# Forgetting attention in a hybrid encoder step: scores of two heads on the two halves of the array rows, transposed, in rounded passes

## The chip, the cores and the metric

The kernel runs on one core of a Trainium2 chip. The metric is the device time of one execution in microseconds (us). The engines are named as in the profile: PE (matrix multiply), PEld (its weight loads), DVE (vector), ACT (activations), POOL, and SP, whose queue issues most transfers.

## The reference

One inference step of a one-layer encoder over 1024 prompt frames and 64 sample frames (width 1024). An RMS norm and one input projection feed two attention groups; their outputs are normalised, projected, added to the input, and followed by a mixture of experts (32 experts, top 2 of one group of 8). All of it is float32. The change touches the first group, forgetting attention with 8 heads of dimension 64:

```python
c_k = jnp.cumsum(logf, axis=1).transpose(0, 2, 1)
sc = (jnp.einsum('bqhd,bkhd->bhqk', qi, k) * SCALE + ci[..., None] - c_k[:, :, None, :])
sc = jnp.where(kpos[None, :] <= qpos[:, None], sc, -jnp.inf)
pr = jax.nn.softmax(sc, axis=-1)
o = jnp.einsum('bhqk,bkhd->bqhd', pr, v)
```

The sample's 64 frames see 256 cached frames and themselves, with the same formula. The outputs of the kernel include the projected K and V.

## The kernel before, in words

Frames are laid out in tiles of 128 partitions: eight prompt tiles (0 to 7), the sample tile (8, half filled), and two tiles of cached keys (9, 10). The kernel has stages that follow one another on PE: input projection in nine column groups of 256 (L1435, three float32r products of high and low parts), forgetting attention (L1484 to L1581), window attention (from L1587), output projection, router, experts.

Forgetting attention loops over pairs of heads (`pe.Fori`, L1570), within a pair over 18 steps, each one query tile of one head. The keys of a head are staged: POOL copies q and k of one head into `qst` and `kst` (L504 to L509), with a 65th column that holds 1/SCALE for q and minus the cumulative log-forget for k, so that the product contains the key's bias. PE transposes them (L1511; the first head L1484), ACT copies the q tiles out of PSUM (L691) and DVE the k tiles (L1039).

A step has six parts. PE multiplies q by all keys up to the diagonal in full float32 (`fqk`, L1530) and adds the causal mask with a bf16 product (L1533); each step alternates between two PSUM couples of banks. DVE takes the negated row maximum (L1047). ACT computes the exponential into `prob` and the row sum (L714). PE transposes each 128x128 block of probabilities (`ftrans`, L1546), DVE copies the first four blocks (L1052) and ACT the others (L724) into `probT`. PE multiplies them by V into one sum over the keys (`fpv`, L1566). DVE scales by the reciprocal of the row sum (L1056, L1059).

Each engine has a queue of its own, in a written order, and waits on semaphores. PE's order within step k is: scores of step k+1, a staging group of the next head, transposes of step k, values of step k-1. The scores of a query tile with n key blocks need 2n instructions' worth of columns, since a float32 product is two instructions.

On SP's queue: cached keys and values arrive once the eighth column group is done (L352 to L355), K and V go out after the projection (L362 to L376), and `w_out` is loaded (L381) when all values have been multiplied and the outputs have left.

Of the kernel before, what the change touches and what calls it, by code (L numbers as in the profile page):

```python
# [6 lines left out]
F32 = mybir.dt.float32  # L7
# [18 lines left out]
SWA = NH * DH + 2 * 2 * DH  # L26
PROJ = QKV + NH + SWA
# [15 lines left out]
def build(nc, t):  # L43

    ctx = ExitStack()
    with ctx:
# [37 lines left out]
        kT = [cut(big, free0 + u * NK * P, NK * P) for u in range(2)]  # L84
        qT = [cut(big, free0 + 2 * NK * P + u * NT * P, NT * P) for u in range(2)]
        at = free0 + 2 * NK * P + 2 * NT * P
        prob = [cut(big, at + u * SEQ, SEQ) for u in range(2)]
        probT = [cut(big, at + (2 + u) * SEQ, SEQ) for u in range(2)]
# [49 lines left out]
        for name in ("e", "s", "r", "a", "hid", "hidT"):  # L138
# [19 lines left out]
        fox_t = fox[:, 0:NT * QKV].rearrange("p (t n) -> p t n", t=NT)  # L158
# [21 lines left out]
        wg_hi = [rounded("wg_hi0", fox_at, NT * QKV, C, WG), rounded("wg_hi1", work_at, 2 * D, C, WG)]  # L180
# [5 lines left out]
        ck = cut(work, at, 2, (NH + 1) * DH)  # L186
        at += 2 * (NH + 1) * DH
        cv = cut(work, at, 2, NH * DH)
        at += 2 * NH * DH
        kst = cut(work, at, NK, DH + 1)  # L190
        at += NK * (DH + 1)
        qst = cut(work, at, NT, DH + 1)
        at += NT * (DH + 1)
        skv = cut(work, at, 2 * 2 * DH)
        at += 2 * 2 * DH
        assert at <= 4 * D
        sqst = cut(work, at, NT, P)
        at += NT * P
        assert at <= 6 * D
        at = NT * QKV + C * WG  # L200
        lz = cut(fox, at, 3 * NT * NH)
        at += 3 * NT * NH
        lsum = cut(fox, at, NK * NH)
        lsum_t = cut(fox, at, NK, NH)
        assert at + NK * NH <= NT * QKV + WSLOT
# [29 lines left out]
        negc = sb("negc", [P, NK * (NH + 1)])  # L235
# [19 lines left out]
            pad_set aug_set kv_staged st_T st_copied_s st_copied_v qk_done nmax_done exp_done pT_a pT_b cp_a cp_b pv_done o_done recip  # L255
# [4 lines left out]
            v_idx v_g v_w v_gT v_gTc v_gu v_e v_s v_hid v_hT v_hTc v_dn v_y v_out experts_done  # L260
# [19 lines left out]
        def wg_dest(g, i):  # L280

            to, c0 = (fox_t, g * WG) if g < FOX_G else (swa_t, (g - FOX_G) * WG)
            return to[:, i, c0:c0 + WG]
# [9 lines left out]
        nblk = [i + 1 for i in range(NP_T)] + [1 + PAST // P]  # L293
        TWO = [i for i in range(NT) if nblk[i] > 4]

        SG = [("q", 0, 4), ("q", 4, 8), ("q", 8, 9), ("k", 0, 4), ("k", 4, 8), ("k", 8, 11)]
        SG_AT = {2: 0, 3: 1, 4: 2, 5: 3, 6: 4, 7: 5}
# [4 lines left out]

        def keytile(i, b):

            return b if i < SAMPLE else [NT, NT + 1, SAMPLE][b]
# [8 lines left out]
        def _(sp):  # L314
# [37 lines left out]
            sp.dma_start(ck[:, :, 0:NH * DH], t["cache_fox_k"].rearrange("l b (t p) h d -> p (l b t) (h d)", p=P)).then_inc(s["cache_in"], 16)  # L352
            sp.dma_start(cv[:, :, :], t["cache_fox_v"].rearrange("l b (t p) h d -> p (l b t) (h d)", p=P)).then_inc(s["cache_in"], 16)
# [6 lines left out]
            for n, name in ((1, "fox_k"), (2, "fox_v")):  # L360
                cols = slice(n * 512, (n + 1) * 512)
                sp.dma_start(t[name + "_prompt"].rearrange("l b (t p) h d -> p (l b t) (h d)", p=P),  # L362
                             fox_t[:, 0:NP_T, cols]).then_inc(s["kv_out"], 16)
                sp.dma_start(t[name + "_sample"].rearrange("l b s h d -> (l b s) (h d)"),
                             fox_t[0:DEC, SAMPLE, cols]).then_inc(s["kv_out"], 16)
# [1526 lines left out]
```

## Time and profile before

| | us |
|---|---|
| median of 3 runs | 1003.92 (1002.94 to 1005.01) |
| the profiled execution's own time | 1010.65 |
| its span in the profile | 1008.8 |
| PE busy / DVE / ACT / POOL in the span | 890.9 / 480.2 / 320.5 / 104.8 |
| forgetting attention, 264 to 472 us | 208 |

The span is the time between the first and the last instruction of the profiled execution. Busy times count overlapping matmuls once. The granted clock is the share of full speed (2.4 GHz) that PE was given; in any moment it is either 1.2 or 2.4 GHz, and a stretch shows the mean.

### The profile page before, as it was taken

How to read it: one execution, taken by the hardware profiler on the slowest of the kernel's cores; microseconds unless marked ns; L12 is line 12 of the kernel's file. 1: busy time of each engine (PE TensorE's matmuls, PEld its weight loads, DVE VectorE, ACT ScalarE, POOL GpSimd, SP SyncE). 2: the span in 40 equal slices, each digit the busy share in tenths (PEclk: the TensorE clock that was granted, in tenths of full speed). 3: DMA queues.
4: the chain of work that ended last, by engine and by line, in shares of the span. 5: the costliest groups of instructions: out<-in, count | busy, mean ns of one | idle time of the engine just before them, and what ended most of it. 6: DMA issues, size and time to landing. Idle time of an engine off the chain costs nothing.

```text
span 1008.8 us, 16897 instructions
## 1 busy us (share of the span) xinstructions
PE 890.9 (88%) x5891; PEld 777.5 (77%) x5891; DVE 480.2 (48%) x1058; ACT 320.5 (32%) x800; POOL 104.8 (10%) x188
## 2 busy tenths in 40 slices
PE   4999999999999999997999989999649999999700
PEld 4999999999787878786989878888537777777400
DVE  4631111111465656666676743342354555544366
ACT  5621111110333443442555733332202222222222
POOL 0000000000000000010000000000132443333200
PEclk9999999999999999999998989999659999999955
DMA  9301111111500000002100042211668999982195
GB/s 260 128 2 42 42 42 42 42 42 48 205 4 1 0 0 0 0 0 90 78 1 0 0 168 84 84 62 73 236 240 309 356 333 323 336 318 101 54 372 179
DMA packets 50699, 118.45 MB, mean 117 GB/s; under 512 B 12960, under 2 KB 22944, under 8 KB 50656
## 3 DMA queue, kind: packets, MB, share of 16 engines
q1 hardware_dynamic: 41440, 100.03, 27.8%
q0 software_dynamic: 9216, 17.85, 5.1%
q8 instruction: 27, 0.44, 0.2%
q14 instruction: 16, 0.13, 0.0%
HBM read 102.93 MB, written 30.64 MB: 132 GB/s over the span
## 4 chain that ended last, share of the span: by engine, by line
PE 83%; DVE 8%; DMA 4%; ACT 2%; issue 2%; SPq 0%; DVEq 0%; POOLq 0%; ACTq 0%; POOL 0%
PE ps L1435 32%; PE ps L1765 11%; PE ps L1530 7%; PE ps L1566 7%; PE ps L1771 6%; PE ps L1546 3%; PE ps L1758 3%; PE ps L1617 3%; PE ps L1650 2%; PE ps L1511 2%; PE ps L1708 2%; DMA out_y_prompt<-big 1%; PE ps L1679 1%; PE ps L1634 1%; DVE big L1403 1%
## 5 line engine op out<-in xcount | busy, mean ns | idle before, releaser
L1435 PE MATMUL ps<-wg_hi,xl 128*128 128x256 f32 x576 | 163.3, 284 | 0.2 <-DVE wg_lo L948 0.2
L1435 PE MATMUL ps<-wg_lo,xh 128*128 128x256 f32 x576 | 163.0, 283 | 0.0
L1435 PE MATMUL ps<-wg_hi,xh 128*128 128x256 f32 x576 | 163.0, 283 | 0.0
L1435 PEld LDWEIGHTS ps<-wg_hi,xl 128*128 128x128 f32 x576 | 110.6, 192 | 0.4 <-issue 0.4
L1435 PEld LDWEIGHTS ps<-wg_lo,xh 128*128 128x128 f32 x576 | 110.6, 192 | 0.0
L1435 PEld LDWEIGHTS ps<-wg_hi,xh 128*128 128x128 f32 x576 | 110.6, 192 | 0.0
L714 ACT ACTIVATE big<-ps,nm 128x384 f32<-128x384 f32 (+7 forms) x72 | 52.1, 723 | 124.5 <-DVE nm L1047 122.9
L1530 PE MATMUL ps<-big 128*128 128x512 f32 (+3 forms) x224 | 85.0, 493 | 1.2 <-DVE big L1039 0.8
L1566 PE MATMUL ps<-fox,big 128*128 x592 | 75.4, 271 | 1.2 <-DVE big L1059 1.2
L1566 PEld LDWEIGHTS ps<-fox,big 128*128 128x128 f32 x592 | 72.0, 192 | 2.9 <-issue 2.8
L1765 PEld LDWEIGHTS ps<-fox,work 128*128 128x128 f32 x320 | 60.8, 190 | 16.8 <-issue 9.6
L1765 PE MATMUL ps<-fox,work 128*128 128x256 f32 x320 | 72.3, 379 | 0.0
L1047 DVE TENSOR_REDUCE nm<-ps 128x1 f32<-128x384 f32 (+7 forms) x72 | 52.9, 735 | 40.1 <-PE ps L1533 39.8
L1298 DVE COPY work<-ps 128x512 f32<-128x512 f32 x32 | 22.1, 691 | 96.7 <-PE ps L1758 96.7
L952 DVE COPY fox<-ps 128x256 f32 (+1 forms) x27 | 11.4, 422 | 101.8 <-PE ps L1435 101.8
L1435 PE MATMUL ps<-w_out_h,oTl 128*128 128x512 f32 x144 | 57.7, 401 | 1.5 <-DVE oTl L1176 1.5
L1435 PE MATMUL ps<-w_out_h,oTh 128*128 128x512 f32 x144 | 56.7, 394 | 0.0
L1435 PE MATMUL ps<-w_out_l,oTh 128*128 128x512 f32 x144 | 56.6, 393 | 0.0
L1530 PEld LDWEIGHTS ps<-big 128*128 128x128 f32 x224 | 38.4, 198 | 17.6 <-issue 17.1
L1546 PE MATMUL ps<-cf,big 128*128 128x128 f32 x312 | 46.8, 276 | 1.1 <-ACT big L714 1.1
L1617 PE MATMUL ps<-big 128*128 128x128 f32 x272 | 42.0, 301 | 4.8 <-DVE big L1086 4.5
L754 ACT ACTIVATE big<-ps,nm 128x256 f32<-128x256 f32 (+1 forms) x72 | 32.7, 460 | 42.5 <-DVE big L1121 25.6
(236 smaller groups left out, 1650.5 us busy)
## 6 DMA issues: line engine op xcount, KB each, us to landing
fox<-in_w_gate SPq DMA_DIRECT2D x20, 512.0 KB, 4.6
fox<-in_w_up SPq DMA_DIRECT2D x20, 512.0 KB, 7.2
fox<-in_w_down SPq DMA_DIRECT2D x20, 512.0 KB, 6.7
work<-in_w_in SPq DMA_DIRECT2D x8, 1024.0 KB, 5.4
fox<-y_rows SPq DMA_DIRECT2D x16, 512.0 KB, 7.0
h_rows<-big SPq DMA_DIRECT2D x9, 512.0 KB, 2.6
work<-in_x_prompt SPq DMA_DIRECT2D x8, 512.0 KB, 7.0
fox<-in_w_out SPq DMA_DIRECT2D x1, 4096.0 KB, 12.8
```

The source lines that it names most:

```text
L714: act.activation(prob[k % 2][:, 0:n], ps[k % 2][:, 0:n], ACT.Exp, bias=nm[:, k % 2:k % 2 + 1], accum_out=rs[:, k % 4:k % 4 + 1]).then_inc( ...
L754: act.activation(sprob[k % 2][:, v, lo:2 * P], bank[k % 3][:, v * 256 + lo:v * 256 + 256], ACT.Exp, bias=nm[:, 2 * (k % 3) + v:1 + 2 * (k ...
L1047: dve.tensor_reduce(nm[:, k % 2:k % 2 + 1], ps[k % 2][:, 0:n], AX.X, ALU.max, negate=True).then_inc(s["nmax_done"], 1)
L1298: dve.tensor_copy(hgT[u][:, 4:8, :], bank[1].rearrange("p (c k) -> p c k", c=4)).then_inc(s["gT_cv"], 1)
L1435: mm = pe.matmul(out, xs[a](c), ws[b](c), start=(c + k == 0), stop=(c == C - 1 and k == 2))
L1530: pe.matmul(ps[k % 2][:, at_:at_ + w], q, kT[u][:, k0:k0 + w], start=(at_ % 512 == 0), stop=False, skip_group_check=True)
L1546: mm = pe.transpose(bank[4 + b // 4][:, (b % 4) * P:(b % 4) * P + P], prob[k % 2][:, b * P:(b + 1) * P], ident)
L1566: mm = pe.matmul(bank[6][:, (k % 2) * DH:(k % 2) * DH + DH], probT[k % 2][:, b * P:(b + 1) * P], v, start=(b == 0), stop=(b == nb - 1))
L1617: pe.matmul(bank[k % 3][:, v * 256 + b * P:v * 256 + (b + 1) * P], sqT[u][:, i * P:(i + 1) * P], skT[v][:, m * P:(m + 1) * P], start=(v == ...
L1758: mm = pe.transpose(bank[c // 4][:, (c % 4) * P:(c % 4) * P + P], src[:, c, :], ident)
L1765: mm = pe.matmul(bank[2 + u][:, 0:2 * FE].rearrange("p (m f) -> p m f", m=2), hgT[u][:, c, :], wv[:, c, :, :], start=(c == 0), stop=(c == ...
L1771: mm = pe.matmul(bank[4 + n], ex["hidT"][u], w[:, 2 * D + 512 * n:2 * D + 512 * n + 512], start=True, stop=True)
```

## The change

Two heads are now handled together, as a pair. Their q and k, which lie side by side in 128 columns of the projection, are transposed together (20 transposes for a pair), so head 0 of the pair lands on partitions 0 to 63 and head 1 on 64 to 127. ACT copies the PSUM tile to a float32r high part (`high`), DVE subtracts it from the PSUM tile to get the low part (`low`). POOL's staging is gone, and with it the 65th column.

For each pair the scores are computed twice.

The natural pass (`scores`, groups n0 to n12 of the list `NAT`) gives only the row maxima: one float32r product of the high parts for each head on its 64 rows, one product with `sel` and `c_rows` that adds the key's bias, and the mask. It writes to banks 0 and 1, which are its only ones. One DVE reduce takes the maxima of both heads (`fmax`). `make_rows` splits the maxima in high and low parts, PE transposes them (`rows_of_maxima`), and DVE spreads them to rows that a product can add.

The transposed pass (`scores_T`) has keys on partitions and queries along the free axis: per step one key tile against up to four query tiles, low x high, high x low, high x high, then a product of ones with the row of maxima, then the mask. Steps alternate between banks 2, 3 and 4, 5. ACT computes the exponential of it straight into `probT`, with the key's bias as its per-partition bias, so no probability is transposed. V has a 65th column of ones, so that `values` also gives the row sums. Its sums for four query tiles and two heads stay in banks 6 and 7 over one half; a pair has two halves (query tiles 0 to 3 and the sample, then 4 to 7), with 7 and 8 steps.

The list `BESIDE` says what stands on PE between the scores of step j+1 and the values of step j: s0 to s5 are staging groups, n0 to n12 natural groups, r0 and r1 the rows of maxima. In the first half these are of the same pair, in the second half of the next pair.

The biases of the keys reach `c_rows` by 16 small transfers from SBUF to SBUF on SP's queue, one for each head and part. K and V leave by one transfer for each tile, V in pieces of 64 elements. The loops of ACT, DVE and PE in this stage are written out instead of `Fori`, those of ACT and DVE for the projection's column groups too. Four small operations of DVE and five of ACT make constants. In the overflow part of the experts some semaphores are merged; no instruction changes there.

The order and the steps:

```diff
+        NPAIR = NH // 2
+        SG = [("k", 0, 4), ("q", 0, 4), ("k", 8, 11), ("q", 8, 9), ("k", 4, 8), ("q", 4, 8)]
+        NAT = [[(3, 0, 512), (8, 8 * P, 384), (2, 0, 384), (1, 0, 256), (0, 0, 128)],
+               [(7, 0, 512), (7, 512, 512), (6, 0, 512), (6, 512, 384), (5, 0, 512), (5, 512, 256), (4, 0, 512), (4, 512, 128)]]
+        STEP = [[(0, 0, 4), (1, 1, 4), (2, 2, 4), (3, 3, 4), (9, 8, 9), (10, 8, 9), (8, 8, 9)],
+                [(m, max(m, 4), 8) for m in range(8)]]
+        N_SG, N_NAT, N_STEP = len(SG), len(NAT[0]) + len(NAT[1]), len(STEP[0]) + len(STEP[1])
+
+        BESIDE = [[["n5", "n6"], ["n7", "n8"], ["n9", "n10"], ["n11", "n12"], ["r1"], [], []],
+                  [["s0", "s1"], ["s2", "s3"], ["s4", "s5"], ["n0", "n1"], ["n2", "n3", "n4"], ["r0"], [], []]]
```

ACT and DVE:

```diff
+            def fexp(n, hp, half, j, step):
+
+                m, a, b = step
+                act.wait_ge(s["fx_st"], n + 1)
+                if n >= 2:
+                    act.wait_ge(s["fx_pv"], n - 1)
+                for v in range(2):
+                    act.activation(probT[2 * (n % 2) + v][:, 0:(b - a) * P], bank[2 + 2 * (n % 2) + v][:, 0:(b - a) * P], ACT.Exp,
+                                   bias=negc_t[:, m, 2 * hp + v:2 * hp + v + 1], scale=SCALE).then_inc(s["fx_exp"], 1)
+
...
+            def fmax(hp, k):
+
+                half, i, k0, w = nat(k)
+                to = top[0][:, :, slot(0, i)] if half == 0 else top[1][:, k0 // 512, :, slot(1, i)]
+                dve.wait_ge(s["fx_nat"], hp * N_NAT + k + 1)
+                dve.tensor_reduce(to, both[:, :, 0:w], AX.X, ALU.max, negate=True).then_inc(s["fx_max"], 1)
+
+            def make_rows(hp, half):
+
+                g = hp * 2 + half
+                nj = 4 if half else 5
+                dve.wait_ge(s["fx_max"], hp * N_NAT + (N_NAT if half else len(NAT[0])))
+                if half:
+                    small_step(dve.tensor_tensor(top[1][:, 0], top[1][:, 0], top[1][:, 1], ALU.min))
+                val = top[1][:, 0] if half else top[0]
+                small_step(dve.tensor_copy(nm_v[:, :, 0:nj], val))
+                small_step(dve.tensor_tensor(nm_v[:, :, 8:8 + nj], val, nm_v[:, :, 0:nj].bitcast(F32), ALU.subtract))
+                dve.sem_inc(s["fx_rc"], 1)
+                dve.wait_ge(s["fx_nmT"], g + 1)
+                if half == 0:
+                    dve.tensor_scalar(row_s, bank[0][:, 0:P], mask8[:, 4:5], None, ALU.mult)
+                dve.tensor_tensor(rows[half].rearrange("p (j q) -> p j q", q=P), bank[0][:, None, 0:P].to_broadcast([P, 4, P]),
+                                  mask8[:, 0:4, None].to_broadcast([P, 4, P]), ALU.mult).then_inc(s["fx_row"], 1)
```

PE, the new functions and the order:

```diff
+            def scores(hp, k):
+                half, i, k0, w = nat(k)
+                u = hp % 2
+                if k == 0:
+                    pe.wait_ge(s["fx_lo"], (hp + 1) * N_SG)
                 else:
+                    pe.wait_ge(s["fx_max"], hp * N_NAT + k)
+                if k == len(NAT[0]):
+                    pe.wait_ge(s["fx_row"], 2 * hp + 1)
+                half_rows = [slice(64 * v, 64 * v + 64) for v in range(2)]
+                for v, r_ in enumerate(half_rows):
+                    pe.matmul(bank[v][:, 0:w], qh[u][r_, i * P:(i + 1) * P], kh[u][r_, k0:k0 + w], start=True, stop=False,
                               skip_group_check=True)
+                dg = i * P - k0
+                ends = 0 <= dg < w
+                for v, r_ in enumerate(half_rows):
+                    mm = pe.matmul(bank[v][:, 0:w], sel[hp][r_, :], c_rows[r_, k0:k0 + w], start=False, stop=not ends,
+                                   skip_group_check=True)
+                if ends:
+                    for v in range(2):
+                        mm = pe.matmul(bank[v][:, dg:dg + P], identb, causal, start=False, stop=True, skip_group_check=True)
+                mm.then_inc(s["fx_nat"], 1)
+            def rows_of_maxima(hp, half):
+                pe.wait_ge(s["fx_rc"], 2 * hp + half + 1)
+                pe.transpose(bank[0][:, 0:P], nm_st.bitcast(F32), ident).then_inc(s["fx_nmT"], 1)
+            def scores_T(n, hp, half, j, step):
+                m, a, b = step
+                u = hp % 2
+                w = (b - a) * P
+                if n >= 2:
+                    pe.wait_ge(s["fx_exp"], 2 * (n - 1))
+                if j == 0:
+                    pe.wait_ge(s["fx_row"], 2 * hp + half + 1)
+                out = [bank[2 + 2 * (n % 2) + v][:, 0:w] for v in range(2)]
+                half_rows = [slice(64 * v, 64 * v + 64) for v in range(2)]
+                for first, (x_, y_) in enumerate([(kl, qh), (kh, ql), (kh, qh)]):
+                    for v, r_ in enumerate(half_rows):
+                        pe.matmul(out[v], x_[u][r_, m * P:(m + 1) * P], y_[u][r_, a * P:b * P], start=(first == 0), stop=False,
+                                  skip_group_check=True)
+                at_ = (a - 4 * half) * P
+                for v, r_ in enumerate(half_rows):
+                    src = row_s[r_, :] if a == SAMPLE else rows[half][r_, at_:at_ + w]
+                    mm = pe.matmul(out[v], ones_r[r_, :], src, start=False, stop=(a != m), skip_group_check=True)
+                if a == m:
+                    for v in range(2):
+                        mm = pe.matmul(out[v][:, 0:P], causal, identb, start=False, stop=True, skip_group_check=True)
+                mm.then_inc(s["fx_st"], 1)
+            def values(n, hp, half, j, step):
+                m, a, b = step
+                if j == 0:
+                    pe.wait_ge(s["fx_o"], 2 * hp + half)
+                for v in range(2):
+                    pe.wait_ge(s["fx_exp"], 2 * n + 1 + v)
+                    val = fox_v[:, m, 2 * hp + v, :] if m < NT else cv[:, m - NT, 2 * hp + v, :]
+                    for i in range(a, b):
+                        at_ = slot(half, i) * HD
+                        mm = pe.matmul(bank[6 + v][:, at_:at_ + HD], probT[2 * (n % 2) + v][:, (i - a) * P:(i - a + 1) * P], val,
+                                       start=(j == 0 and i == a), stop=(m == i), skip_group_check=True)
+                mm.then_inc(s["fx_pv"], 1)
+            pe.wait_ge(s["pad_set"], 4)
+            pe.wait_ge(s["sel_set"], NPAIR + 1)
+            pe.wait_ge(s["crow_in"], 16 * 2 * NH)
+            for k in range(len(NAT[0])):
+                scores(0, k)
+            rows_of_maxima(0, 0)
+            pe.wait_ge(s["evac_v"], EVAC_V)
+            pe.wait_ge(s["evac_s"], EVAC_S)
+            order = list(steps())
+            scores_T(*order[0])
+            for n, hp, half, j, step in order:
+                if n + 1 < len(order):
+                    scores_T(*order[n + 1])
+                for kind, k, to in beside(hp, half, j):
+                    if kind == "s":
+                        stage(to, k)
+                    elif kind == "n":
+                        scores(to, k)
                     else:
+                        rows_of_maxima(to, k)
+                values(n, hp, half, j, step)
```

SP's queue, the key biases:

```diff
+            sp.wait_ge(s["pad_set"], 2)
+            sp.wait_ge(s["c8_hi"], 1)
+            sp.wait_ge(s["c8_lo"], 1)
+            for h in range(NH):
+                for b, part in enumerate((ch, cl)):
+                    r_ = 64 * (h % 2) + 2 * (h // 2) + b
+                    sp.dma_start(c_rows[r_:r_ + 1, :].bitcast(F32).rearrange("a (t c) -> a t c", c=P),
+                                 part[h * NK:(h + 1) * NK, :].bitcast(F32)).then_inc(s["crow_in"], 16)
```

## Rows read from the trace of the kernel before

**Rows 1.** The page: busy time, share of the span and instructions; and the clock in 40 slices.

```profile
PE 890.9 (88%) x5891; PEld 777.5 (77%) x5891; DVE 480.2 (48%) x1058; ACT 320.5 (32%) x800; POOL 104.8 (10%) x188
...
PEclk9999999999999999999998989999659999999955
```

**Rows 2.** Table of windows: stretch, length, each engine's busy us (instructions), clock, DMA share, GB/s.

```profile
264.00:472.00 208.00, 201.86 (x1392) 162.77 (x1392) 128.59 (x311) 82.31 (x203) 13.82 (x34) 0.98 0.07 24
472.00:583.00 111.00, 98.83 (x771) 92.14 (x771) 82.08 (x256) 63.34 (x227) 5.08 (x8) 0.92 0.11 42
...
735.00:1008.00 273.00, 205.54 (x968) 157.52 (x968) 141.25 (x268) 66.86 (x157) 78.59 (x128) 0.86 0.73 264
```

**Rows 3.** Timeline of PE, 276 to 288 us: start, duration, engine, line, operation, count.

```profile
276.01 1.72 PE L1530 MATMUL ps<-big 128*128 128x512 f32 x4
...
279.79 1.94 PE L1530 MATMUL ps<-big 128*128 128x512 f32 x4
281.56 0.22 PE L1533 MATMUL ps<-cb 128*128 128x128 bf16 x1
281.62 0.60 PE L1511 MATMUL ps<-cf,work 128*65 128x128 f32 x4
...
285.20 1.04 PE L1546 MATMUL ps<-cf,big 128*128 128x128 f32 x8
286.07 1.67 PE L1566 MATMUL ps<-fox,big 128*128 x14
```

**Rows 4.** Chain of waits: start, duration, what, with its count.

```profile
234.16 20.18 PE ps L1435 x168
...
600.91 10.90 PE ps L1435 x48
```

**Rows 5.** Timeline of all engines, two moments; idle time and its releaser in brackets.

```profile
410.00 0.22 PE L1533 MATMUL ps<-cb 128*128 128x128 bf16 x1
...
410.26 1.22 DVE L1047 TENSOR_REDUCE nm<-ps 128x1 f32<-128x1024 f32 x1 [1.20 <-PE ps L1533]
...
467.91 0.28 DVE L1059 TENSOR_SCALAR big<-ps,rc 128x64 f32 x1 [1.21 <-PE ps L1566]
...
468.34 1.97 PE L1566 MATMUL ps<-fox,big 128*128 x16 [0.31 <-DVE big L1059]
```

**Rows 6.** DVE by line and shape, 264 to 472 us: count, busy us, mean ns, idle before.

```profile
L1047 DVE TENSOR_REDUCE nm<-ps 128x1 f32<-128x1024 f32 x8 | 9.8, 1224 | 9.6 <-PE ps L1533 9.6
...
L1047 DVE TENSOR_REDUCE nm<-ps 128x1 f32<-128x768 f32 x8 | 7.7, 958 | 6.6 <-PE ps L1533 6.6
...
L1047 DVE TENSOR_REDUCE nm<-ps 128x1 f32<-128x512 f32 x8 | 5.5, 691 | 1.2 <-PE ps L1533 1.2
...
L1047 DVE TENSOR_REDUCE nm<-ps 128x1 f32<-128x256 f32 x8 | 3.4, 424 | 1.8 <-PE ps L1533 1.4
```

**Rows 7.** ACT by line and shape, 264 to 472 us.

```profile
L714 ACT ACTIVATE big<-ps,nm 128x384 f32<-128x384 f32 x16 | 9.3, 581 | 17.4 <-DVE nm L1047 17.4
...
L714 ACT ACTIVATE big<-ps,nm 128x512 f32<-128x512 f32 x8 | 5.5, 687 | 8.1 <-DVE nm L1047 8.1
L724 ACT ACTIVATE big<-ps 128x512 f32<-128x512 f32 x8 | 4.8, 598 | 0.0
...
L714 ACT ACTIVATE big<-ps,nm 128x256 f32<-128x256 f32 x8 | 3.8, 474 | 12.2 <-DVE nm L1047 10.6 <-PE ps L1546 1.6
...
L714 ACT ACTIVATE big<-ps,nm 128x128 f32<-128x128 f32 x8 | 2.9, 368 | 26.3 <-DVE nm L1047 26.3
```

**Rows 8.** Timeline of SP's queue: transfers that it issues.

```profile
235.23 0.43 SPq L355 DMA_DIRECT2D work<-in_cache_swa_v  x1
262.00 0.33 SPq L359 DMA_DIRECT2D g<-in_g_ffn_norm  x1
...
263.50 1.90 SPq L362 DMA_DIRECT2D out_fox_v_prompt<-fox  x1
```

**Rows 9.** The page's line on DMA packets.

```profile
DMA packets 50699, 118.45 MB, mean 117 GB/s; under 512 B 12960, under 2 KB 22944, under 8 KB 50656
```

More of the change, by code:

```diff
@@ L292, in build, with steps, beside, nat @@
         NS = len(STEPS)
[L293 to L297, printed above, removed]
+        NPAIR = NH // 2
[7 more added lines that the diff above has]
+                  [["s0", "s1"], ["s2", "s3"], ["s4", "s5"], ["n0", "n1"], ["n2", "n3", "n4"], ["r0"], [], []]]
+        def steps():
+            n = 0
+            for hp in range(NPAIR):
+                for half in range(2):
+                    for j, step in enumerate(STEP[half]):
+                        yield n, hp, half, j, step
+                        n += 1
+        def beside(hp, half, j):
+            for what in BESIDE[half][j]:
+                at_ = hp + half
+                if at_ < NPAIR:
+                    yield what[0], int(what[1:]), at_
+        def nat(n):
+            half = 0 if n < len(NAT[0]) else 1
+            return (half,) + NAT[half][n - half * len(NAT[0])]
+        def slot(half, i):
+            return 4 if i == SAMPLE else i - 4 * half
         SSG = [(0, 4), (4, 8), (8, 9)]
@@ L737, in stage_sq @@
+            fexp(*next(steps()))
+            order = list(steps())
+            for n, hp, half, j, step in order:
+                if n + 1 < len(order):
+                    fexp(*order[n + 1])
+                for kind, k, to in beside(hp, half, j):
+                    if kind == "s":
+                        high(to, k)
             def stage_sq(g3, u, gi, bk=7):
@@ new lines, in _ @@
+            for k in range(len(NAT[0])):
+                fmax(0, k)
+            make_rows(0, 0)
+            for n, hp, half, j, step in steps():
+                for kind, k, to in beside(hp, half, j):
+                    if kind == "s":
+                        low(to, k)
+                    elif kind == "n":
+                        fmax(to, k)
+                    else:
+                        make_rows(to, k)
+                if j == len(STEP[half]) - 1:
+                    fnorm(hp, half)
@@ L1490, in _ @@
                 product(k // 2 + 1, k, i).then_inc(s["proj_done"], 1)
+                if i == 3:
+                    pe.wait_ge(s["c_ready"], 1)
+                    pe.transpose(bank[1][0:NH * NK, 0:P], c8[:, :], ident).then_inc(s["c8_T"], 1)
                 if i >= 6:
[L1492 to L1512 removed]
@@ L1570, in _ @@
[L1570 to L1584 removed]
+                    if i == 6:
+                        pe.wait_ge(s["c8_lo"], 1)
+                        pe.wait_ge(s["cache_in"], 16 * 5)
@@ new lines, in _ @@
+            pe.wait_ge(s["pad_set"], 4)
+            pe.wait_ge(s["sel_set"], NPAIR + 1)
+            pe.wait_ge(s["crow_in"], 16 * 2 * NH)
+            for k in range(len(NAT[0])):
+                scores(0, k)
+            rows_of_maxima(0, 0)
+            pe.wait_ge(s["evac_v"], EVAC_V)
+            pe.wait_ge(s["evac_s"], EVAC_S)
+            order = list(steps())
+            scores_T(*order[0])
+            for n, hp, half, j, step in order:
+                if n + 1 < len(order):
+                    scores_T(*order[n + 1])
+                for kind, k, to in beside(hp, half, j):
+                    if kind == "s":
+                        stage(to, k)
+                    elif kind == "n":
+                        scores(to, k)
+                    else:
+                        rows_of_maxima(to, k)
+                values(n, hp, half, j, step)
```

411 lines of the change are left out of this document (159 added, 252 removed).

## The prediction

> **What bounds the kernel now.** The page's busy line and clock line come first: the matmul engine (PE) is busy 88% of the span and no other engine reaches half of it [rows 1]. The table of windows cuts the span into stages: the forgetting attention, which is what changes, lies from 264 to 472 us, and there PE is busy 201.9 of 208 us at a granted clock of 0.98, against DVE 128.6 and ACT 82.3 [rows 2]. So in this stage only two things count: time for which PE is occupied, and time for which it must wait. Everything of ACT, DVE, POOL and the DMA queues counts only through a wait of PE.
>
> A busy figure of PE overlaps itself, since a matmul shows 0.27 us or more while the next one starts much sooner. I therefore price matmuls by their pitch. Eight probability transposes take 1.04 us in all, the first one's 0.27 included, so each further one costs (1.04 - 0.27)/7 = 0.11 us; 14 value matmuls take 1.67 us, also 0.11 each; a full float32 product is two instructions, so a 128-key block of values is 0.22 us; the score line grows from 1.72 to 1.94 us for 128 more keys, 0.22 us a block; the mask matmul lasts 0.22 us but the next one starts 0.06 us after it [rows 3]. The rounded (float32r) products of the projections run at 20.18/168 = 0.120 us for 256 columns, and at 10.92/48 = 0.2275 us for 512 [rows 4]. I take 0.174 us for 384, and for 128 the 0.11 us which every 128-column weight load shows as its floor.
>
> Check on the stage of before: one head has 39 blocks of 128x128 keys by queries, so 39 x 0.22 scores + 9 x 0.06 masks + 39 x 0.11 probability transposes + 20 x 0.11 staging transposes + 39 x 0.223 values = 24.3 us, a pair of heads 48.6; the stage measured 208/4 = 52.0 a pair, 3.4 us of it waits. This is the sum that the new one has to beat.
>
> **The change, for one pair of heads.** Staging: 20 transposes serve both heads, 2.2 us (before: 4.4). The probability transposes (78 x 0.11 = 8.6 us) go, with their copies on DVE and ACT. The values stay: 156 instructions of 0.1115, 17.4 us, only their output is 65 columns for 64. Masks double to 36 at 0.06 = 2.2 us. Two transposes of the maxima are 0.2.
>
> Scores are now computed twice. The natural pass (for the maxima alone) has 13 groups with widths 512 x6, 384 x3, 256 x2, 128 x2: 6 x 0.2275 + 3 x 0.174 + 2 x 0.12 + 2 x 0.11 = 2.35 us for one matmul each, times 2 (scores, then the key bias), times 2 heads = 9.4 us. The transposed pass has 15 steps, 512 x6, 384 x2, 256 x2, 128 x5: 2.50 us, times 4 (three rounded products and the row of maxima), times 2 heads = 20.0 us. Together 29.4 us if each matmul waits its turn. The two heads of a pair, however, lie on array rows 0-63 and 64-127, write to different banks and stand next to each other in the program. No row of this trace has a matmul on half the rows, so the price is bounded: below, both heads in one pitch, 29.4/2 = 14.7 us; above, 29.4. Between them, if the products run side by side but the two weight loads follow one another (2 x 0.11 = 0.22 us a couple): 36 couples at 0.2275 and 50 at 0.22 = 19.2 us. I take 17.0, the middle of 14.7 and 19.2, because disjoint rows leave nothing in the products to share, and only the loads are in doubt. The page TensorEngine Tiling (Array Packing), Key Properties, of the Trainium skill says that tiles on different rows load weights and multiply in parallel; no run here shows it yet, and by it the term would be the 14.7.
>
> Waits inside the pair. The natural pass owns one couple of banks, and PE stands at a natural group until DVE has reduced the previous one. Where two stand in one slot of the written order, nothing covers that. One wait: from the last matmul's issue to the reduce 0.26 us, the reduce itself (now two banks at once, so 2 x 512 = 1024 elements, 1.22 us), and 0.15 us from DVE's end to PE, less the pitch already counted: 1.55 us [rows 5, 6]. By the order this happens before n6, n8, n10, n12 and n1 (1024 elements), n3 (768: 0.96, so 1.29) and n4 (512: 0.69, so 1.02): 5 x 1.55 + 1.29 + 1.02 = 10.1 us. Behind the waiting group on PE stand the values of the current step, so nothing else can run. The one-block steps at the end of the first half add about 0.3: PE has 0.45 + 0.55 us of other work for two exponentials of 0.37 [rows 7] and their hand-overs. 10.4 us.
>
> The other engines stay under PE. ACT: 30 exponentials, 12 x 0.69 + 4 x 0.58 + 4 x 0.47 + 10 x 0.37 = 16.1, and six high parts at 0.6 or less: 19.4 us [rows 7]. DVE: reduces 12.4, low parts about 3.7, norms and rows about 5: 21 us. The wait of staging group 2 for the low part of group 0 comes out covered: about 3.1 us of ACT and DVE against 3.5 us of PE work (transposes 0.9, values 1.8, next scores 0.9). The norm of a half (about 1.4 us) lies under the next scores and two groups.
>
> Pair: 2.2 + 0.2 + 2.2 + 17.4 + 17.0 + 10.4 = 49.4 us; four pairs 197.6.
>
> Beside them. At the start nothing covers the natural groups of pair 0, nor the row chain after them: about 4.6 us more (1.3 for one more bare wait, 2.7 for maxima, transpose and rows, 0.6 for the first exponential). Its staging ends with a copy and then a subtraction where a single copy stood: 1.2 us. At the end the norm has three multiplications of four blocks, 0.8 us. Together 6.6. The 16 small row transfers are issued on SP from about 249 us (their source is ready after five products of 24 x 0.12 us from 234 us on) to 256 us at 0.4 us each, or to 265 us and later where the queue is full and an issue takes 1 to 1.9 us [rows 8]; I cost them at nothing, since the last product runs to 262 us, and at 4 us if the cover fails. The output of V is now 256-byte pieces, over 8,700 where the whole kernel had 12,960 packets under 512 B [rows 9]; only the load of w_out waits for it, 200 us later. POOL's staging goes, which PE did not wait for.
>
> Turning between half-row and full-row products. PE does this about 18 times a pair each way where no wait hides it, 144 in all. The rows show that a matmul's tail past its pitch is 0.22 - 0.06 = 0.16 us [rows 3]; between full-row forms this costs nothing, so the bounds are 0 and 0.16 us, 0 to 23 us in all. I take 0.07, since part of the tail must lie under the next weight load: 10 us. The Trainium skill's page TensorEngine Tiling (Array Packing), Key Properties, also says that a change of tiling mode drains the engine; by it the term would be the 23 us. This is the rule that speaks against the change, and nothing in this trace agrees or disagrees.
>
> Stage: 197.6 + 6.6 + 10 = 214.2 us against 208, so +6.2. The profiled execution of before took 1010.65 us around a span of 1008.8; it would become 1016.9. It lies 6.7 us over the median of the three runs, and I carry the difference over to the median: 1003.9 + 6.2 = 1010 us.
>
> **Rivals.**
> B, faster: loads as well as products of the two heads run side by side, and turning costs nothing. Scores 14.7: stage 4 x 47.1 + 6.6 = 195 us, 13 less than before: 991 us. For it: the two loads touch disjoint rows as the products do, and full-row forms follow each other without a gap in [rows 3]. Against it: every load form here has a floor of 0.11 us, whatever its matmul. It decides for faster as soon as a couple of 128-column products has a pitch near 0.11 us and turning stays under 0.04 us.
> C, no overlap: a half-row matmul costs its full turn. Scores 29.4: 4 x 12.4 = 50 us over the forecast, 1060 us. For it: no row shows an overlap. Against it: separate rows, separate banks, alternating order.
> D, the clock: PE now stands 42 us of the stage in gaps of 1 to 1.6 us. The expert stage, PE 75% busy, has a granted clock of 0.86, the window attention with 89% has 0.92 [rows 2]. At 0.86 the 172 us of PE work in the stage grow by 172 x (0.98/0.86 - 1) = 24 us: 1034 us. Against it: the idle stretches there are longer than any here.
>
> **How the numbers follow.** Forecast 0.45, B 0.28, C 0.17, D 0.10. The forecast's own range takes scores 14.7 to 19.2 and turning 0 to 23 us, without both low ends together: 1000 to 1032. The range takes in B with a few us below it and C's centre: 988 to 1063. This kernel can be told from no change beyond 0.2%, 2 us. Faster: B and 0.06 of the forecast, 0.34; same 0.10; slower 0.56.
>
> **What would show it.** Couples of half-row matmuls that start within some ns of each other confirm the overlap; their pitch at 128 columns (0.11 or 0.22) tells B from the forecast; a step from the first half-row product after values later than 0.11 us shows the turning. PE's waits for the reduce should number 28 with about 40 us in total. The stage should be 214 us long with PE idle some 45 of it. The prediction is wrong if the couples don't overlap (stage over 250), if the waits for the reduce are much shorter than 1.5 us, or if the clock of the stage falls under 0.95.

## The result, and the profile after

The changed kernel takes 1111.0 us (median of 4 runs, 1105.5 to 1114.9) against 1004.5 us of the kernel before (median of 4 runs), a ratio of 1.105 (1.098 to 1.111). The forecast was 1010 us and its range ended at 1063: it was wrong. The profiled execution took 1112.8 us, its span is 1110.9 us.

The page of the changed kernel, to be held against [rows 1]; each digit of the clock line is one slice of 28 us:

```profile
PE 966.6 (87%) x6024; PEld 833.4 (75%) x6024; DVE 428.0 (39%) x880; ACT 306.9 (28%) x744; POOL 91.2 (8%) x154
...
PEclk9999999997575675565558998999985999999965
```

The table of windows for the changed kernel: a stretch of the attention stage at full clock, one at the low clock, two longer ones in which PE never waits, and in the last row the whole stage:

```profile
325.00:328.00 3.00, 3.00 (x27) 2.92 (x28) 1.17 (x2) 2.24 (x4) 0.00 (x0) 1.00 0.03 5
334.00:337.00 3.00, 3.00 (x17) 2.25 (x16) 0.00 (x0) 0.05 (x1) 0.00 (x0) 0.50 0.00 0
343.00:355.00 12.00, 12.00 (x65) 10.46 (x64) 0.98 (x3) 1.47 (x4) 0.00 (x0) 0.50 0.01 1
545.00:578.00 33.00, 33.00 (x158) 28.96 (x158) 0.00 (x0) 7.55 (x14) 0.00 (x0) 0.50 0.00 1
262.00:578.00 316.00, 278.08 (x1522) 219.29 (x1522) 78.15 (x128) 66.78 (x139) 0.00 (x0) 0.58 0.06 17
```

Before, the stage had 208 us at a clock of 0.98 [rows 2]; now it has 316 us at 0.58. The stages behind it last 537 us before and 532 after. So all of the loss is in this stage, and PE runs at 1.2 GHz in most of it; the run with filled waits below shows that nearly all of the loss is this clock. The clock comes back four times, near 318, 356, 390 and 469 us, and after 484 us no more in this stage, though PE is busy without a break in its last 33 us (545 to 578 us, at 0.50). That is why a table of busy time misleads here.

The waits of PE for the reduce in the changed kernel (us in total, times, longest) are 29, the 28 of the forecast and the one more at the start. They sum to 34.9 us where 41.7 were forecast:

```profile
PE ps L1584 <- DVE rs L1093: 21.2, 16, 1.3
PE ps L1584 <- DVE nm L1093: 13.7, 13, 1.3
```

The timeline of PE in the changed kernel shows the same products at both clocks. The two heads' halves are one line, x2:

```profile
325.86 1.90 PE L1635 MATMUL ps<-fox,big 128*128 128x65 f32 x16
327.69 0.50 PE L1614 MATMUL ps<-qh,kl 64*128 64x512 f32 x2
328.03 0.40 PE L1614 MATMUL ps<-ql,kh 64*128 64x512 f32 x2
328.26 0.40 PE L1614 MATMUL ps<-qh,kh 64*128 64x512 f32 x2
...
341.94 3.62 PE L1635 MATMUL ps<-fox,big 128*128 128x65 f32 x16
...
347.05 2.66 PE L1635 MATMUL ps<-fox,big 128*128 128x65 f32 x12
349.64 0.47 PE L1614 MATMUL ps<-qh,kl 64*128 64x128 f32 x2
349.91 0.41 PE L1614 MATMUL ps<-ql,kh 64*128 64x128 f32 x2
350.13 0.41 PE L1614 MATMUL ps<-qh,kh 64*128 64x128 f32 x2
```

At full clock a couple of 512-column halves has a pitch of 0.23 us (328.03 to 328.26), that of one 512-column product [rows 4]: they run side by side. A run of 16 values takes 1.90 us there and 3.62 us at the low clock, a pitch of 0.11 and 0.21 us. Products of 100 columns in place of 65 take nearly the same time in the runs below (16 in 1.98 us at full clock). So the columns do not set this pitch; the load of 128 columns of weights, which is the same for both, is what is left. Such products are called load-bound here, and sparse, because the array has columns to multiply in only a part of each pitch.

### The profile page after: what moved, and what is told of

It is laid out like the page before. It is cut to its first block, busy times and chain, and to the rows that moved or that the text cites. A ratio compares the mean times of both kernels' runs of the same rounds, so it can differ in the third digit from the quotient of the medians.

```text
span 1110.9 us, 15975 instructions
## 1 busy us (share of the span) xinstructions
PE 966.6 (87%) x6024; PEld 833.4 (75%) x6024; DVE 428.0 (39%) x880; ACT 306.9 (28%) x744; POOL 91.2 (8%) x154
## 4 chain that ended last, share of the span: by engine, by line
PE 83%; DVE 9%; DMA 3%; issue 2%; ACT 2%; SPq 1%; DVEq 0%; POOLq 0%; ACTq 0%; POOL 0%
PE ps L1502 29%; PE ps L1635 10%; PE ps L1843 10%; PE ps L1614 6%; PE ps L1849 5%; PE ps L1584 3%; PE ps L1836 3%; PE ps L1695 3%; PE ps L1728 2%; DVE rs L1093 2%; PE ps L1619 2%; PE ps L1786 1%; PE ps L1589 1%; DVE nm L1093 1%; SPq L412 1%
## 5 line engine op out<-in xcount | busy, mean ns | idle before, releaser
L757 ACT ACTIVATE big<-ps,negc 128x512 f32<-128x512 f32 (+3 forms) x120 | 58.1, 535 | 247.7 <-PE ps L1622 169.3
L1635 PE MATMUL ps<-fox,big 128*128 128x65 f32 x592 | 118.2, 375 | 0.0
L1635 PEld LDWEIGHTS ps<-fox,big 128*128 128x128 f32 x592 | 114.0, 291 | 4.6 <-issue 3.9
L1584 PE MATMUL ps<-kh,qh 64*128 64x512 f32 (+3 forms) x104 | 32.5, 622 | 36.9 <-DVE rs L1093 21.2
L1093 DVE TENSOR_REDUCE rs<-ps 128x2 f32<-128x1024 f32 (+3 forms) x32 | 32.8, 1026 | 75.5 <-PE ps L1589 55.1
L1584 PEld LDWEIGHTS ps<-kh,qh 64*128 64x128 f32 x104 | 14.0, 266 | 54.2 <-DVE rs L1093 32.1
L983 DVE COPY fox<-ps 128x256 f32<-128x256 f32 x27 | 11.4, 423 | 100.8 <-PE ps L1502 100.8
L679 ACT ACTIVATE fox<-ps 128x256 f32<-128x256 f32 x27 | 10.4, 386 | 108.2 <-PE ps L1502 108.2
```

What stands on the lines that cost most here:

```text
L757: act.activation(probT[2 * (n % 2) + v][:, 0:(b - a) * P], bank[2 + 2 * (n % 2) + v][:, 0:(b - a) * P], ACT.Exp, bias=negc_t[:, m, 2 * hp ...
L1093: dve.tensor_reduce(to, both[:, :, 0:w], AX.X, ALU.max, negate=True).then_inc(s["fx_max"], 1)
L1584: pe.matmul(bank[v][:, 0:w], qh[u][r_, i * P:(i + 1) * P], kh[u][r_, k0:k0 + w], start=True, stop=False, skip_group_check=True)
L1635: mm = pe.matmul(bank[6 + v][:, at_:at_ + HD], probT[2 * (n % 2) + v][:, (i - a) * P:(i - a + 1) * P], val, start=(j == 0 and i == a), sto ...
```

## The experiments

Theory A: uncovered waits pull the clock down, and the sparse products (values of 65 columns, couples of 128) keep it down. Theory B: products on half the rows, or the mix as such, do it. These kernels answer a question about time; some of them leave out a part of the computation, as said there. In the code, `...` marks lines left out. Each window row shows the stage: length, busy us of PE, PEld, DVE, ACT and POOL, clock, DMA share, GB/s.

**Shorter waits, same products.**

```diff
-                dve.tensor_reduce(to, both[:, :, 0:w], AX.X, ALU.max, negate=True)
+                dve.tensor_reduce(to, both[:, :, 0:32], AX.X, ALU.max, negate=True)
```

> Everything of the changed kernel stays, but DVE reduces only the first 32 columns of each natural group, so PE's 28 uncovered waits shrink from about 1.3 us of idle PE to about 0.4 us (the maxima then come from fewer keys, which a softmax forgives). Theory A (the clock falls because of the gaps, and once it is down the long load-bound value runs keep it down): without gaps of 1.3 us the clock stays at 0.95 or more, and the stage falls from 316 to 175 to 190 us, the whole to 975 to 990 us. Theory B (products on half the rows, or the mix as such, lower the clock, the gaps do not matter): clock of the stage stays near 0.58, only the gaps go, 25 to 30 us: about 1083 us.

Measured 991.8 us beside 1004.4, just over the range of theory A. The waits for the reduce fall from 34.9 to 9.3 us, and the clock is back with PE's products unchanged:

```profile
262.00:455.00 193.00, 181.25 (x1524) 141.07 (x1524) 39.47 (x128) 66.06 (x139) 0.00 (x0) 0.96 0.10 28
```

**No natural pass.** This kernel leaves out the products and the reduction of the first pass, and the staging of the maxima with them, so the rows of maxima stay zero. The transposes of the (empty) maxima stay, with waits of their own for the staged keys and the rows, which are not shown:

```diff
             def scores(hp, k):
+                return
...
             def fmax(hp, k):
+                return
...
-                small_step(dve.tensor_copy(nm_v[:, :, 0:nj], val))
-                small_step(dve.tensor_tensor(nm_v[:, :, 8:8 + nj], val, nm_v[:, :, 0:nj].bitcast(F32), ALU.subtract))
```

> The natural pass is left out altogether (PE's groups n0 to n12 and DVE's reduces; the rows of maxima are zeros). Nothing is left on PE but staging, transposed scores and values, with no gap. At full clock one pair is 2.2 + 0.2 + 1.1 + 17.4 + 10 + about 3 of turning = 34 us, the stage 140 us. Theory A: clock near 1, stage 140 us, whole about 935 to 945 us. Theory B (half-row products and narrow values lower the clock by themselves): clock 0.5 to 0.65, stage 220 to 270 us, whole 1020 to 1070 us.

Measured 938.5 us, stage 141 us. Couples of half-row products, values and staging hold the full clock (1.00 in the whole stage) when nothing interrupts them; B as a statement on all half-row products falls.

```profile
262.00:403.00 141.00, 139.68 (x1244) 119.68 (x1243) 24.15 (x55) 65.48 (x138) 0.00 (x0) 1.00 0.14 38
370.00:403.00 33.00, 32.81 (x293) 28.10 (x291) 2.83 (x8) 14.51 (x30) 0.00 (x0) 1.00 0.01 1
```

The second row, the last 33 us of this stage, is to be held against the last 33 us of the changed kernel (545 to 578 us). The products that end the stage are the same in both, without a wait; here they run at 1.00 and there at 0.50. What differs is the clock at which they were reached: they held the full clock, and they did not bring it back.

**Filled waits.** Two waits at the start of the stage move ahead of the first fillers, which is not shown:

```diff
+            FILL = 20
...
+                    if fill:
+                        for _ in range(FILL):
+                            pe.matmul(bank[6][:, 384:512], identb, identb, start=False, stop=True, skip_group_check=True)
                     pe.wait_ge(s["fx_max"], hp * N_NAT + k)
...
+                        if j == 0 and last == "n":
+                            pe.wait_ge(s["fx_o"], 2 * hp + half)
+                        scores(to, k, last == "n")
```

> The changed kernel with 20 small full-row bf16 products of 128 columns (0.056 us each at full clock, 1.1 us in all) on PE in each uncovered wait before a natural group; their sum is never read. They lie in time that PE waits anyway. Theory A: the clock stays up, stage 205 to 225 us, whole 1000 to 1020 us. Theory B: no change in the clock (0.58); the whole 1110 us or more.

Measured 1016.2 us beside 1004.4: 580 more products and 95 us less time than the changed kernel. The natural groups come no earlier, PE is only kept busy until they may start, and the clock does not fall. This is also the test of the forecast's sum, which had no term for the clock: 214 us of stage were forecast, 217.7 are there, and the whole is 1016 us where 1010 was forecast. So even at full clock this order of the products is not faster than the kernel before.

```profile
262.00:479.70 217.70, 212.27 (x2104) 172.03 (x2104) 77.49 (x128) 65.78 (x139) 0.00 (x0) 0.99 0.09 25
```

**Wider values, all waits kept.**

```diff
-                    val = fox_v[:, m, 2 * hp + v, :] if m < NT else cv[:, m - NT, 2 * hp + v, :]
+                    c0 = (2 * hp + v) * HD - 35
+                    val = (fox_t[:, m, 2 * NH * DH + c0:2 * NH * DH + c0 + 100] if m < NT else
...
-                        at_ = slot(half, i) * HD
-                        mm = pe.matmul(bank[6 + v][:, at_:at_ + HD], probT[2 * (n % 2) + v][:, (i - a) * P:(i - a + 1) * P], val,
+                        at_ = slot(half, i) * 100
+                        mm = pe.matmul(bank[6 + v][:, at_:at_ + 100], probT[2 * (n % 2) + v][:, (i - a) * P:(i - a + 1) * P], val,
```

> The changed kernel with all its gaps, but the value products move 100 columns in place of 65 (35 columns of neighbouring data whose sums are never read). Their pitch is set by the weight load, 0.11 us at the high clock and 0.21 at the low one, so the extra columns are free in time. Theory A: the gaps still pull the clock down, but a busier value run lets it return sooner: clock of the stage 0.7 to 0.9, whole 1020 to 1070 us. If the narrow value runs play no part: clock 0.58, whole 1111 us. Theory B with half-row products as the culprit: 1111 us too.

Measured 1057.8 us: 35 useless columns in each value product, the same waits (34.9 us), and 53 us less, since the clock comes back more often. The sparse values are a part of what kept it down, not all of it: the mean is 0.77.

```profile
262.00:524.00 262.00, 224.22 (x1524) 174.15 (x1524) 77.92 (x128) 66.38 (x139) 0.00 (x0) 0.77 0.08 21
```

**Another order on PE** (the list `BESIDE`, whose change is not shown, and the positions):

```diff
+                items = list(beside(hp, half, j))
+                if items:
+                    work_on(*items[0], False)
                 if n + 1 < len(order):
                     scores_T(*order[n + 1])
-                for kind, k, to in beside(hp, half, j):
...
-                values(n, hp, half, j, step)
+                values(n, hp, half, j, step, items[1] if len(items) > 1 else None)
```

> The whole computation of the changed kernel, only PE's order differs: of two natural or staging groups of a slot, one stands ahead of the next transposed scores and one between the values of the two heads, so each has 0.9 to 1.9 us of work behind it, and at most two stand in a slot. The uncovered waits of a pair fall from 10.1 us by my count to about 4 us, none over 0.8 us. Theory A (gaps pull the clock down): clock of the stage 0.95 or more, stage 217.7 - 25 = about 190 us, whole 975 to 990 us. If the total of idle time and not the single gap decides, the clock still falls in part: 1000 to 1060 us.

Measured 1025.2 us (1020.7 to 1029.7; ratio 1.020, 1.009 to 1.031), over the range of theory A and within that of its alternative. The clock is down in the first 20 us of the stage, where the groups of the first pair still stand bare with waits up to 1.3 us. Behind them the waits for the reduce are 0.4 us and less, but the clock still fell, three times, each time in the one-block steps at the end of a first half; the last time, near 449 us, it stayed down to the end of the stage. The first of the three:

```profile
337.00:342.00 5.00, 4.30 (x44) 3.48 (x40) 2.96 (x3) 1.25 (x4) 0.00 (x0) 1.00 0.00 0
342.00:347.00 5.00, 4.76 (x33) 4.01 (x33) 1.81 (x6) 1.25 (x4) 0.00 (x0) 0.63 0.02 5
347.00:352.00 5.00, 5.00 (x23) 3.62 (x24) 1.18 (x4) 1.26 (x2) 0.00 (x0) 0.50 0.00 0
```

So waits of 1.3 us are not needed for a fall: the ones ahead of this one are 0.26 to 0.38 us.

**The same order with short fillers:**

```diff
+                    if fill:
+                        for _ in range(10 if hp or k > 4 else 20):
+                            pe.matmul(bank[6][:, 384:512], identb, identb, start=False, stop=True, skip_group_check=True)
```

> The kernel with the spread order, and 10 small full-row bf16 products (0.56 us) ahead of the natural groups that can still wait (20 at the start). Theory A: the clock is at 0.99 whatever the spread order gives by itself; where the wait is shorter than the filler, the filler costs its difference: 980 to 995 us, 0 to 10 us over the spread order alone if that one keeps its clock, and below it if it does not.

Measured 1009.3 us, ratio 1.003 (0.998 to 1.009): clock 0.99, but the fillers were longer than what was left to fill, and cost more than I allowed.

```profile
262.00:473.50 211.50, 204.07 (x2004) 167.62 (x2004) 77.52 (x129) 66.23 (x139) 0.00 (x0) 0.99 0.10 26
```

**Waits in the kernel before.**

```diff
                         fqk(it, k + 1)
+                        pe.wait_ge(s["nmax_done"], it * NS + (k + 2))
```

> The kernel before, with one wait added on PE in each of its 72 steps of forgetting attention: after the scores of step k+1 it waits until DVE has their maximum. All products are on full rows. The wait is 0.35 to 1.4 us by the size of the reduce (0.29 to 1.22 us), 72 x 0.85 = about 60 us at full clock. Theory A: the clock falls here too, so the whole rises well over the 60 us, to 1090 to 1180 us. Theory B (half-row products were needed for the fall): clock stays at 0.95 or more, whole about 1055 to 1070 us.

Measured 1093.2 us, 88 more, of which 64.8 are the new waits themselves. PE idles 69 of 300 us, nearly twice the 38 of the changed kernel, and yet:

```profile
264.00:563.70 299.70, 230.51 (x1391) 173.18 (x1389) 132.87 (x311) 85.96 (x203) 13.39 (x33) 0.91 0.05 17
```

The total fits A's lower end, its reason does not: the clock falls for 9 to 16 us at a time, about once a pair of heads, and comes back, where the changed kernel is down for 22 us to more than 90 at a time. The falls begin where one pair ends and the next starts with narrow scores (128 and 256 columns); where the wide full float32 scores follow the waits, the clock stays at 1.00. Idle time alone does not decide.

**The halves in turn.** The kernel without the natural pass, with the loop over heads outside the loop over products:

```diff
-                for first, (x_, y_) in enumerate([(kl, qh), (kh, ql), (kh, qh)]):
-                    for v, r_ in enumerate(half_rows):
+                for v, r_ in enumerate(half_rows):
+                    for first, (x_, y_) in enumerate([(kl, qh), (kh, ql), (kh, qh)]):
```

The product with the row of maxima moves into the same loop.

> The kernel without the natural pass, but the four products of head 0 of a transposed step now stand ahead of the four of head 1, so that neighbours share their rows and cannot run side by side; all else is the same. If side by side was worth half of the score time, a pair grows by about 10 us: 938.5 + 40 = 978 us, with the clock still at 0.95 or more. If the products of the two heads never overlapped, the time stays at 938.5 us.

Measured 941.2 us. My expectation, 978 us, took products that stand one behind the other in the program to run one behind the other, and was wrong, see the last section. What it gives for no overlap at all, 938.5 us, is ruled out by the next two runs.

**Both heads on the same rows,** in the kernel without the natural pass; the scores of head 1 are left out, since head 0's are computed twice:

```diff
+                half_rows = [slice(0, 64)] * 2
```

> The kernel without the natural pass, in which the score products of head 1 take their operands from rows 0 to 63 as well (so head 1's scores are those of head 0: that part is left out). No product has a partner on other rows. If rows 0 to 63 and 64 to 127 really run side by side in the changed kernel, as its trace shows, each couple now costs two turns: 60 steps, a pair 20.0 - 10.0 = 10 us more, 938.5 + 40 = 978 us. If a half-row product is simply twice as fast by itself, the time stays at 938.5 us; this also tells why it made no difference in which order the two heads' products stood.

Measured 1125.5 us, 187 more and not 40. PE is busy all the time, at the low clock throughout:

```profile
262.00:592.00 330.00, 328.26 (x1244) 283.35 (x1244) 25.04 (x56) 67.01 (x139) 0.00 (x0) 0.50 0.06 16
```

Without any wait for another engine after the first 20 us, this mix, in which each score product has half of the rows to itself, never brings it up.

**The same with values of 100 columns,** by the diff of the wider values above.

> The kernel whose head 1 takes its score operands from rows 0 to 63 too (head 1's own scores are left out), 1125 us at a clock of 0.50 in all of the stage, now with value products of 100 columns. If sparsely streaming products held the clock down, the denser values bring it back, wholly or in part: at full clock the stage is 141 + 40 = 181 us and the whole 978 us; half of the time at the low clock would give about 1050 us. If products on half the array rows by themselves hold it down, the time stays at 1125 us.

Measured 1038.0 us, near my half-and-half case: 240 us of stage at 0.73. So half-row products by themselves do not hold the clock down either. It comes back three times, and falls three times more, always in the one-block steps at the end of a first half, where PE has no wait at all and couples of 128 columns stand beside the values. The stage, and the first of these falls:

```profile
262.00:502.00 240.00, 238.87 (x1243) 203.11 (x1243) 24.43 (x55) 65.78 (x138) 0.00 (x0) 0.73 0.08 22
332.00:342.00 10.00, 10.00 (x74) 9.14 (x74) 0.69 (x1) 2.71 (x8) 0.00 (x0) 0.90 0.01 2
342.00:352.00 10.00, 10.00 (x28) 7.15 (x28) 1.17 (x4) 2.04 (x5) 0.00 (x0) 0.50 0.00 0
```

So where the heads do not run side by side, the clock falls even without a wait. The timeline gives the price of a couple without overlap at full clock: 0.23 us for 2 x 256 columns and 0.22 for 2 x 128, where couples on separate rows need 0.12 and 0.11 (the run with filled waits; the 0.11 is in the next section).

```profile
388.84 0.40 PE L1615 MATMUL ps<-ql,kh 64*128 64x256 f32 x2
389.07 0.40 PE L1615 MATMUL ps<-qh,kh 64*128 64x256 f32 x2
...
391.50 0.38 PE L1615 MATMUL ps<-ql,kh 64*128 64x128 f32 x2
391.72 0.39 PE L1615 MATMUL ps<-qh,kh 64*128 64x128 f32 x2
```

**A version under the kernel before: spread order and wide values,** the two diffs above together; the value tile starts 35 columns early, and the last 65 are read. This kernel computes all that the changed one does.

> The spread order (whose clock fell to 0.5 three times, each time in the one-block steps at the end of a first half, where it still has gaps of 0.3 us and 65-column values) together with the values of 100 columns, which are free in time. Refined theory A (gaps and sparsely streaming products act together; either removed keeps the clock up): clock of the stage 0.95 or more, stage about 217.7 - 40.6 + 16.2 = 193 us, whole 988 to 995 us, under the kernel before. If only the gaps count, the clock stays at 0.82 as in the spread order and the whole at 1020 to 1030 us.

Measured 999.8 us (998.2 to 1002.2), ratio 0.994 (0.992 to 0.996): a little under the kernel before, and 5 us over my range. From 282 us on the clock is 1.00; in the first 20 us of the stage, with the bare groups of the first pair, it is 0.57, and my 193 us of stage had no term for that.

```profile
262.00:464.20 202.20, 184.28 (x1524) 143.76 (x1524) 77.47 (x129) 66.22 (x139) 0.00 (x0) 0.96 0.10 27
```

**And fillers at the start of the stage,** ahead of the natural groups of the first pair and around the transpose of its maxima (the second place is not shown):

```diff
+                    if hp == 0 and k < len(NAT[0]):
+                        for _ in range(20):
+                            pe.matmul(bank[7][:, 384:512], identb, identb, start=False, stop=True, skip_group_check=True)
```

> The kernel with spread order and wide values, whose clock was 1.00 from 282 us on but 0.5 to 0.7 between 262 and 282 us, where the five natural groups of pair 0 and their rows stand with nothing beside them. Here 20 small full-row bf16 products stand in each of those waits, and 36 around the transpose of the maxima. The waits themselves stay, so only the slow clock of these 20 us can be won: the products there are some 12 us, half of it 4 to 8 us. Whole 990 to 996 us, clock of the stage 0.99. If the slow start costs nothing, because waits rule it, the time stays at 999 us.

Measured 997.7 us (992.4 to 998.9), ratio 0.992 (0.989 to 0.994). The clock of the first 20 us is 0.91 instead of 0.57, but the interval of the time overlaps with the one without fillers; that the clock of these 20 us matters is not shown.

## Why the prediction was wrong

The step that failed is the clock. The sum that gave 214 us prices every product at the pitch of full clock and has no term for a fall; the clock stands only in rival D, and there it failed in its size. I said that at a clock of 0.86 the 172 us of PE work would grow by 24 us, gave it 0.10, and set against it that the idle stretches of the expert stage are longer than any here. The 0.86 was the mean of another stage, with other products. Here the mean was 0.58, and the clock costs about 95 us: 1111.0 less the 1016.2 of the filled kernel, whose clock is 0.99. The mechanism was named, but its size was off by a factor of four: D's 1034 us lay inside the range, and nothing in the prediction reached 1111. In its place the runs show two things that act together: the waits, of 1.3 us and in the spread kernel even of 0.3, and the value products of 65 columns. Shorter waits alone give back 119 us, of which 26 are the waits themselves; wider values alone 53. A third, the couples of 128 columns, is argued and not shown: in the spread kernel and in the one with both heads on the same rows and wide values, the falls lie where they stand. What I overlooked is that the clock depends on what went before: the same products at the end of the stage held 1.00 in the kernel without the natural pass and stayed at 0.50 in the changed one. In three of its four pairs the clock of the changed kernel came back in the second half, whose steps have staging transposes beside them; the last pair has none, and it stayed down.

The rest of the sum held. Couples have a pitch of 0.11 us for 128 columns and 0.23 for 512, so the score term is rival B's 14.7 us a pair and not my 17.0. The Trainium skill, TensorEngine Tiling (Array Packing), Key Properties, says so for loads and products on different rows, and the trace agrees. The timeline of PE in the filled kernel, at full clock:

```profile
341.27 0.40 PE L1594 MATMUL ps<-c_rows,sel 64*128 64x512 f32 x2
341.60 1.29 PE L1583 MATMUL ps<-cb 128*128 128x128 bf16 x20
...
343.55 1.06 PE L1640 MATMUL ps<-fox,big 128*128 128x65 f32 x8
344.53 0.33 PE L1619 MATMUL ps<-qh,kl 64*128 64x128 f32 x2
344.70 0.28 PE L1619 MATMUL ps<-ql,kh 64*128 64x128 f32 x2
344.81 0.27 PE L1619 MATMUL ps<-qh,kh 64*128 64x128 f32 x2
```

Turning costs more than my 0.07 us, and on the way in as much as the bound of 0.16: the first couple after values takes 0.17 instead of 0.11, and the step from the last value to it (344.53 - 343.55 - 7 x 0.11 = 0.21) 0.10 more; on the way out it is 0.33 instead of 0.23. That is 0.26 us for in and out; 72 times, an estimate from these two places, it makes 19 us, where I had 10. The Trainium skill, TensorEngine Tiling (Array Packing), Key Properties, also says that a change of mode drains the engine; a cost of this size at each turn agrees with it. The score term was 9 us too high over the four pairs and the turning 9 us too low, so that this part of the sum came out right is luck.

The waits for the reduce: 4 x 10.1 + 1.3 = 41.7 us were forecast, 34.9 are in the trace, none longer than 1.3 us where I had 1.55. The chain at the start waits 2.0 us for the last of the 16 row transfers, within the 4 I gave if the cover fails. Nothing speaks of V's small output pieces: PE never waits for them.

Rival C is refuted by the pitch. B's mechanism was right for the couples; that the whole gains by it shows only in the spread order with the clock up (999.8 us), since the filled kernel in the order of the change takes 1016.2.

What stays open: how much of the loss the couples of 128 columns cause by themselves, as no run widened them, and what exactly the clock answers to.

## What to carry to other kernels

A kernel that fills PE to 97% at full clock has the clock as a second resource: before a change puts waits and sparse products next to each other, ask what brings the clock back once it has fallen, and give a low clock in the whole stage (here a factor of nearly two on its PE time) a case of its own. When the clock line drops and busy time does not, fill the waits for one run: it separates the clock from the waits themselves. Widening a load-bound product cost nothing here from 65 to 100 columns, and was worth 53 us.

## What the runs showed of the hardware

Products on separate row halves ran side by side even where their order in the program is not alternating. In the kernel with the halves in turn, all four products of head 0 stand ahead of those of head 1, and the timeline still shows both heads in each line:

```profile
312.80 0.51 PE L1615 MATMUL ps<-qh,kl 64*128 64x512 f32 x2
313.14 0.40 PE L1615 MATMUL ps<-ql,kh 64*128 64x512 f32 x2
313.37 0.40 PE L1615 MATMUL ps<-qh,kh 64*128 64x512 f32 x2
313.60 0.41 PE L1618 MATMUL ps<-rows,ones_r 64*128 64x512 f32 x2
313.94 0.32 PE L1634 MATMUL ps<-fox,big 128*128 128x65 f32 x1
```

Eight products of 512 columns take 1.14 us to the start of the next value product; one after the other they would take 8 x 0.2275 = 1.82. The kernel takes 941.2 us beside 938.5. The Trainium skill, TensorE: Matmul & The Clock Gate, Part 3, says that matmuls start and end strictly in program order; across row halves these rows differ, and the measurement decides.

A busy engine is not enough for the full clock: the mix with one half of the rows at a time, PE busy 328 of 330 us, ran at 1.2 GHz all through. With values of 100 columns in place of 65 the same mix had 0.73, and fell from 2.4 to 1.2 GHz three times with PE busy and no wait ahead of the fall.
